# Up projection of a hybrid encoder layer: the moving activations read, and the output columns written, in descending order of tokens

## What is computed

```python
def rmsnorm(x, g):
    xf = x.astype(jnp.float32)
    y = xf * lax.rsqrt(jnp.mean(xf * xf, axis=-1, keepdims=True) + EPS)
    return (y * g.astype(jnp.float32)).astype(x.dtype)

def conv_glu_ffn(h, w_up, w_conv, w_down):
    up = causal_dwconv(h @ w_up, w_conv)
    g, u = jnp.split(up, 2, axis=-1)
    return (jax.nn.silu(g) * u) @ w_down

x = x + conv_glu_ffn(rmsnorm(x, norm_ffn[l]), ffn_up[l], ffn_conv[l], ffn_down[l])
```

## Time and profile before

| | us |
|---|---|
| median of three runs | 2098.74 |
| the profiled execution, its own time | 2098.79 |
| its span, first to last instruction | 2096.6 |
| busy: PE / DVE / ACT / POOL | 2052.9 / 1229.7 / 895.7 / 34.0 |
| line 1735, first to last start | 1339.7 to 1831.2 |
| mean granted TensorE clock, share of full | 0.992 |

### The profile page before, as it was taken

One profiled execution on the slowest core, in us unless ns is written; L12 is line 12 of the kernel. 1 busy time (PEld: TensorE's weight loads), 2 busy tenths in 40 slices (PEclk: granted clock), 3 DMA queues, 4 the chain that ended last, 5 costly groups with the idle time before them and its releaser, 6 DMA issues.

```text
span 2096.6 us, 36640 instructions
## 1 busy us (share of the span) xinstructions
PE 2052.9 (98%) x15803; PEld 1983.2 (95%) x15803; DVE 1229.7 (59%) x1312; ACT 895.7 (43%) x864; POOL 34.0 (2%) x44
## 2 busy tenths in 40 slices
PE   5999999999999999999999999999999999999998
PEld 5999999999999999999999999888888888899998
DVE  5477644543544457577474445677877777744443
ACT  4444433344446443355444434544444444433332
POOL 2000000000000000000000000000000000000000
PEclk8999999999999999999999999999999999999999
DMA  7555444366455865656565355656555655556563
GB/s 220 162 177 190 137 133 134 111 205 200 151 172 176 299 198 189 213 161 190 177 194 163 121 160 166 218 178 200 188 179 193 200 181 180 181 199 194 188 195 125
DMA packets 358511, 377.43 MB, mean 180 GB/s; under 512 B 11913, under 2 KB 354723, under 8 KB 357123
## 3 DMA queue, kind: packets, MB, share of 16 engines
q1 hardware_dynamic: 354771, 353.36, 52.9%
q0 software_dynamic: 3632, 22.42, 2.9%
HBM read 364.75 MB, written 11.01 MB: 179 GB/s over the span
## 4 chain that ended last, share of the span: by engine, by line
PE 95%; DVE 2%; ACT 1%; issue 1%; DMA 0%; POOL 0%; SPq 0%; DVEq 0%; ACTq 0%
PE bank L1701 22%; PE bank L1703 22%; PE bank L1702 22%; PE bank L1735 15%; PE bank L1737 8%; PE bank L1912 1%; PE bank L1859 1%; DVE w_lo L974 1%; PE bank L2115 1%; PE bank L2096 1%; ACT w_hi L457 0%; DVE tmp L1018 0%; DVE x_home L1024 0%; PE bank L1846 0%; PE bank L1778 0%
## 5 line engine op out<-in xcount | busy, mean ns | idle before, releaser
L974 DVE TENSOR_TENSOR w_lo<-raw,w_hi 128x2048 fp32r<-128x2048 f32 (+1 forms) x352 | 763.8, 2170 | 630.3 <-ACT w_hi L457 629.8
L457 ACT ACTIVATE w_hi<-raw 128x2048 fp32r<-128x2048 f32 (+1 forms) x354 | 644.1, 1820 | 1105.8 <-PE bank L1703 827.3
L1701 PE MATMUL bank<-x_home,w_hi 128*128 128x256 f32 x2304 | 653.1, 283 | 18.3 <-DVE x_home L1024 15.2
L1703 PE MATMUL bank<-x_home,w_lo 128*128 128x256 f32 x2304 | 648.0, 281 | 0.0
L1702 PE MATMUL bank<-x_home,w_hi 128*128 128x256 f32 x2304 | 646.9, 281 | 0.0
L1735 PE MATMUL bank<-x_home,w_hi 128*128 128x512 f32 x1408 | 488.7, 391 | 3.6 <-DVE x_home L1583 2.2
L1701 PEld LDWEIGHTS bank<-x_home,w_hi 128*128 128x128 f32 x2304 | 436.2, 189 | 21.0 <-issue 13.3
L1702 PEld LDWEIGHTS bank<-x_home,w_hi 128*128 128x128 f32 x2304 | 437.0, 190 | 0.2
L1703 PEld LDWEIGHTS bank<-x_home,w_lo 128*128 128x128 f32 x2304 | 436.1, 189 | 0.0
L1737 PE MATMUL bank<-x_home,w_lo 128*128 128x256 f32 x1408 | 397.6, 282 | 0.0
L1735 PEld LDWEIGHTS bank<-x_home,w_hi 128*128 128x128 f32 x1408 | 264.4, 188 | 59.4 <-DVE xT L988 1.7
(11 more groups left out here) (279 smaller groups left out, 2182.9 us busy)
## 6 DMA issues: line engine op xcount, KB each, us to landing
raw<-in_w_in SPq DMA_DIRECT2D x53, 2048.0 KB, 8.6
raw<-in_ffn_up SPq DMA_DIRECT2D x44, 2048.0 KB, 8.0
raw<-in_ffn_down SPq DMA_DIRECT2D x32, 1408.0 KB, 6.5
raw<-in_xa_wkv SPq DMA_DIRECT2D x16, 2048.0 KB, 8.9
raw<-in_w_br SPq DMA_DIRECT2D x8, 2048.0 KB, 8.3
raw<-in_w_out SPq DMA_DIRECT2D x8, 2048.0 KB, 8.7
raw<-in_xa_wq SPq DMA_DIRECT2D x8, 2048.0 KB, 8.1
raw<-in_xa_wo SPq DMA_DIRECT2D x8, 2048.0 KB, 8.1
```

The costliest lines, as they stand in the source:

```text
L457: return nc.scalar.activation(out_, in_, func, **kw)
L974: tt(split_out(w_lo, kind, half), halves(raw, kind, half, par), split_out(w_hi, kind, half).bitcast(f32), ALU.subtract).then_inc(lo_ready, 1)
L1701: mm(o, w[0], x[0], start=start, stop=False)
L1703: return mm(o, w[1], x[0], start=False, stop=stop)
```

## The change

The two matmuls of UP read the last index of the moving operand, the tokens, from 255 down to 0, and write the output columns in the same order, so that each token's result goes to the same column as before. In the first matmul the two parts still come one after the other: part 0 from token 255 to 0, then part 1 from 255 to 0. Weights, buffers, semaphores, banks, transfers and the other engines' code are as they were.

```diff
                         o = up_bank(par, half)
-                        mm(o[:, :].rearrange("p (j s) -> p j s", j=2), w_hi[:, half, k * P:(k + 1) * P], acts[:, :, k, :],
+                        mm(o[:, :].rearrange("p (j s) -> p j s", j=2)[:, :, ::-1], w_hi[:, half, k * P:(k + 1) * P], acts[:, :, k, ::-1],
                            start=k == 0, stop=False)
-                        last = mm(o[:, SEQ:2 * SEQ], w_lo[:, half, k * P:(k + 1) * P], acts[:, 0, k, :], start=False, stop=k == KC - 1)
+                        last = mm(o[:, SEQ:2 * SEQ][:, ::-1], w_lo[:, half, k * P:(k + 1) * P], acts[:, 0, k, ::-1], start=False, stop=k == KC - 1)
```

## The result

| | before | changed |
|---|---|---|
| median, us (7 runs each) | 2098.41 | 2103.14 |
| lowest to highest, us | 2096.54 to 2099.78 | 2102.61 to 2104.48 |
| profiled execution, its own time / span, us | 2098.79 / 2096.6 | 2104.21 / 2102.0 |

The account below looks back on a forecast made before the run. The prediction took TensorE's pace, without slack in the Up projection, as the bound. Its four points summed to 0 us, so the forecast was 2098.7 us, with a range of 2085.2 to 2116.7 us.

Parts of the forecast that it names:

- What bounds the kernel: Up projection: TensorE is busy for all 470 us, so its pace counts; VectorE is the next bound, at 78% of the stage.
- Point 1: Lines 1735 and 1737 reading the moving operand backwards: taken as 0, from line 1912's broken reads costing about 1 ns.
- Point 2: Both Up matmuls writing output columns backwards: taken as 0, with half rate as the upper end.
- Point 3: Line 1735's output in two runs where there was one: between 0 and 6.4 ns a pair, taken as 0.
- Up's surcharge: Time of an Up matmul pair above one column a cycle at 2.4 GHz: 26.7 ns a pair, 37.6 us over 1408 pairs.
- Point 4: ScalarE (line 912) and VectorE (line 1603) wait for whole units, so order inside a matmul reaches nobody; no wait added.
- Rival 1: Lines 1735 and 1737 need two cycles a column when descending: 450.6 us more, giving 2549 us; chance 0.16.
- Rival 2: Line 1735's second output run costs 6.4 ns a pair, 9.0 us, giving 2107.7 us; chance 0.14.
- the sign I had named for it: In Up, line 1735 would show 0.235 us with line 1737 unmoved.
- My rule: In Up, if only line 1735 moves, its runs are the cause; if both move in proportion to columns, the direction.
- Rival 3: Up's reversed reads meet the weight loads elsewhere, so the surcharge falls 6.4 ns a pair, 9.0 us, to 2089.7 us; chance 0.18.
- the forecast of no change: Whole kernel stays at 2098.7 us; chance 0.52, of which 0.02 is for the reversal being dropped when operands are laid out.

## Why the prediction was wrong, point by point

- **What bounds the kernel** was right. TensorE had no slack in Up, and 4.4 ns a pair became 6.2 us. VectorE's share of the stage only fell.
- **Point 1, the price of reading backwards, taken as 0,** is the step that failed. With the operand at byte 32 it is 4.4 ns a pair, 6.2 us, and it is nothing at byte 64: what I had taken for a property of the read alone depends on where the weights lie. The rows I took it from, of broken reads in line 1912, told only of gaps, and in matmuls whose pitch would have hidden even a doubling. I had written that down and taken 0 all the same.
- **Point 2, writing backwards at 0,** was right, shown by the run that turns round the writes alone.
- **Point 3, two runs in the output at 0,** was right. Its upper end was built on a wrong reading: the 6.4 ns between Up's surcharge and Down's are not the input's second run.
- **Point 4, nothing waits for the order inside a matmul,** was right.
- **Rival 1, half rate,** is excluded: the pair rose by 1.3%, not by 92%.
- **Rival 2** gave nearly the right time (2107.7 us), and the sign I had named for it: line 1735 up, line 1737 unmoved. Its cause is refuted. My rule that a move of line 1735 alone points to its runs was no test, since the run with only the reads turned round has the same split (233.1 and 118.1 ns). The split between the lines says little, as the run with line 1737 alone has it.
- **Rival 3** had the mechanism, with the wrong sign. It said that the place of reads relative to the weight loads matters by 3.2 ns a matmul, and that a stream running the other way meets them elsewhere. I priced only the better meeting and left the worse one to half a sentence beside rival 2. The ascending read already had the best distance of the two I tried for it, and the descending one lost at all six. Its 3.2 ns came from one pace of Down and one of the query projection, and those rows don't show a placing: Down itself had 120.0 ns a matmul earlier in the same trace. So it is probably luck that its 6.4 ns are close to the 6.6 ns that byte 64 costs.
- **The numbers.** 2103.14 us lies inside the range; the forecast of no change, with 0.52, was wrong, and slower had 0.30. With rival 3 priced to both sides its chance should have been split at least evenly.

## What to carry to other kernels

In a stage where TensorE streams without a gap, the place of the moving operand relative to the weights is worth trying in steps of 16 bytes: byte 64 in place of 32 cost this kernel 0.42% with no other edit. A change of direction undid a good place here (4.4 ns a pair), so a layout that has been chosen for it has to be tried again after a change of direction or of what is allocated ahead, and the distance kept when something is inserted. To find the cause of a few nanoseconds, change one side at a time (read or write, weights or activations) and count pairs over a long window; one line's own pitch misleads. Compare the timed executions too, since a trace shows one pace of possibly several.

## What the runs showed that I had not expected

- A descending write into PSUM costs TensorE nothing (346.7 ns a pair), nor does a second run in the output or in the input.
- The pairs took few values: 346.7, 351.1, 353.3 and 357.8 ns are 2.2 ns apart or a multiple of it. Only byte 28, with 348.6, doesn't fit. Besides the two with moved weights, five descending kernels at five places and one ascending ended at the same 353.3 ns, with four different splits. Why is open.
- The slowest pair of all, 357.8 ns, is that of the descending read off a multiple of 16 bytes; the ascending one, with 348.6, is faster than an aligned one at byte 64. The Trainium skill (SBUF — State Buffer, Specifications (TRN2)) has lines of 16 bytes in SBUF, with a penalty for each crossing to a new one; such an operand touches 65 lines for 256 columns in place of 64, in either direction alike. That would explain a small price of its own. These two runs can't show it, as their distance to the weights changed as well.
- A stage can have several paces with the same instructions at the same places. Down had 120.0 ns a matmul at first before and 116.7 in the changed kernel. With line 1735 alone descending, one execution took 2097.0 us and four took 2105.2 to 2107.7. And in the mixer the two kernels with moved weights are alike, their edits of Up aside, yet in the same 20 us they have 172 matmuls (ascending Up) and 179 (descending Up), where the kernel before has 174. In that order:

```profile
710.00:730.00 20.00, 20.00 (x172) 1.00 0.94 329
```

```profile
710.00:730.00 20.00, 20.00 (x179) 1.00 1.00 351
```

```profile
710.00:730.00 20.00, 20.00 (x174) 1.00 0.97 342
```

So the distance alone doesn't fix the pace there, and a pace better than that of before exists. What selects it is open. In Up every trace keeps one pace from 1360 to 1820 us, and where nothing else was moved the timed executions agree with it, but for those with line 1735 alone.
